# Weight splits ahead of the activation work at each feed-forward start, and two norms moved, in a two-block transformer kernel on one core

## The reference

```python
x = x + 0.5 * swiglu(rmsnorm(x, ffn1_norm[l]), w_ffn1_in[l], w_ffn1_out[l])   # hidden width 2816
x = x + mixer(rmsnorm(x, mix_norm[l]))          # block 1: MLA + HGRN2 + memory attention, gated
x = x + 0.5 * swiglu(rmsnorm(x, ffn2_norm[l]), w_ffn2_in[l], w_ffn2_out[l])   # block 2: RWKV-7 + retention
```

## Time and profile before

| | |
|---|---|
| median of 3 runs | 2368.36 us (2367.09 to 2368.44) |
| the profiled execution | 2367.09 us, of which the span of the instructions 2365.3 |
| TensorE busy | 2348.6 us |
| weight loads of TensorE (they overlap the matmuls) | 2300.9 us |
| VectorE busy | 1570.5 us |
| ScalarE busy | 1201.0 us |
| GpSimd busy | 116.5 us |
| transfers | 406.92 MB, mean 172 GB/s |

### The profile page before, as it was taken

The page is one execution under the profiler, slowest core; times in us unless marked ns, Lnnn a source line. Parts: engine busy times, 40 slices in busy tenths (PEclk is TensorE's granted clock), DMA queues, the critical chain, the costliest instruction groups (busy, mean ns, idle before and its releaser), DMA issues.

```text
span 2365.3 us, 52326 instructions
## 1 busy us (share of the span) xinstructions
PE 2348.6 (99%) x23022; PEld 2300.9 (97%) x23022; DVE 1570.5 (66%) x1416; ACT 1201.0 (51%) x1214; POOL 116.5 (5%) x74
## 2 busy tenths in 40 slices
PE   9999999999999999999999999999999999999998
PEld 8999999999999999999999999999999999999998
DVE  6766777865675568777556656866656656866655
ACT  5545655544454456565445444736445444735443
POOL 0000251000000003500000000000000000000000
PEclk9999999999999999999999999999999999999999
DMA  8656454555555554445655565513655664513653
GB/s 287 204 194 184 131 163 134 188 193 192 184 196 195 195 174 143 144 143 173 207 192 176 196 195 165 183 39 126 208 188 179 207 195 164 184 39 126 202 190 106
DMA packets 322781, 406.92 MB, mean 172 GB/s; under 512 B 6480, under 2 KB 291152, under 8 KB 322384
## 3 DMA queue, kind: packets, MB, share of 16 engines
q1 hardware_dynamic: 321488, 400.58, 52.3%
q10 hardware_dynamic: 1152, 4.22, 0.5%
HBM read 403.72 MB, written 1.05 MB: 171 GB/s over the span
## 4 chain that ended last, share of the span: by engine, by line
PE 92%; ACT 3%; DVE 3%; issue 1%; DMA 0%; SPq 0%; DVEq 0%; ACTq 0%
PE ps L339 83%; PE ps L344 8%; ACT w_hi L298 1%; DVE w_lo L303 1%; PE ps L1487 0%; DMA raw<-in_w_ffn_in 0%; DVE pad L1992 0%; DVE x_hl L392 0%; PE ps L2203 0%; ACT coef L1873 0%; ACT x_hl L366 0%; DVE x L2191 0%; DVE rms L2019 0%; ACT k_t L1132 0%; ACT kk L1842 0%
## 5 line engine op out<-in xcount | busy, mean ns | idle before, releaser
L339 PE MATMUL ps<-x_hl,w_hi 128*128 128x256 f32 x7808 | 1344.0, 277 | 2.4 <-issue 0.9
L303 DVE TENSOR_TENSOR w_lo<-raw,w_hi 128x2048 fp32r<-128x2048 f32 x383 | 881.3, 2302 | 466.5 <-ACT w_hi L298 465.8
L339 PEld LDWEIGHTS ps<-x_hl,w_hi 128*128 128x128 f32 x7808 | 1177.4, 188 | 7.0 <-issue 3.2
L339 PE MATMUL ps<-x_hl,w_lo 128*128 128x256 f32 x3904 | 1078.8, 276 | 0.0
L298 ACT CAST w_hi<-raw 128x2048 fp32r<-128x2048 f32 x383 | 731.1, 1911 | 602.6 <-PE ps L339 591.1
L339 PEld LDWEIGHTS ps<-x_hl,w_lo 128*128 128x128 f32 x3904 | 732.9, 188 | 0.0
L339 PE MATMUL ps<-h_hi,w_lo 128*128 128x256 f32 x1408 | 390.3, 277 | 0.0
L339 PE MATMUL ps<-h_hi,w_hi 128*128 128x256 f32 x1408 | 390.3, 277 | 0.0
L339 PE MATMUL ps<-h_lo,w_hi 128*128 128x256 f32 x1408 | 390.2, 277 | 0.0
L339 PEld LDWEIGHTS ps<-h_hi,w_lo 128*128 128x128 f32 x1408 | 265.2, 188 | 0.0
L339 PEld LDWEIGHTS ps<-h_hi,w_hi 128*128 128x128 f32 x1408 | 265.2, 188 | 0.0
(11 more groups left out here) (455 smaller groups left out, 2471.0 us busy)
## 6 DMA issues: line engine op xcount, KB each, us to landing
raw<-in_w_ffn_in SPq DMA_DIRECT2D x87, 1024.0 KB, 5.1
raw<-in_w_in SPq DMA_DIRECT2D x74, 1024.0 KB, 5.4
raw<-in_w_ffn_out SPq DMA_DIRECT2D x44, 1024.0 KB, 4.9
raw<-in_ffn_w_gate SPq DMA_DIRECT2D x44, 1024.0 KB, 5.3
raw<-in_ffn_w_up SPq DMA_DIRECT2D x44, 1024.0 KB, 5.3
raw<-in_ffn_w_down SPq DMA_DIRECT2D x44, 1024.0 KB, 4.9
raw<-in_w_out SPq DMA_DIRECT2D x16, 1024.0 KB, 5.2
raw<-in_w_mem_kv SPq DMA_DIRECT2D x8, 1024.0 KB, 5.0
```

What stands on the lines that cost most here:

```text
L303: nc.vector.tensor_tensor(w_lo[:, slot, :], raw[:, slot, :], w_hi[:, slot, :].bitcast(F32), ALU.subtract).then_inc(lo_ready, 1)
L339: mm = nc.tensor.matmul(out_ap, l, r, start=first and n == 0, stop=last and n == 2, skip_group_check=True)
```

## The change

Five edits of order; no arithmetic is changed.

1. ScalarE, start of each feed-forward stage: the casts of units (q+1, 0) and (q+1, 1) stand ahead of the silu and of the cast of `hid`, in place of behind them.
2. VectorE, the same place: the low split of (q+1, 0) stands ahead of `scale_silu`, that of (q+1, 1) ahead of `product`. Both stood behind `product`.
3. VectorE, end of stage 6: the low split of the next stage's second unit stands ahead of the updates of x, in place of behind them.
4. TensorE, stage 6: the norm's matmuls stand ahead of the fifth row chunk of the second projection, as in the other stages; they stood ahead of the third.
5. TensorE, mixers of block 2: the norm's matmuls stand ahead of the projection U_K, in place of in its middle.

```diff
             nc.scalar.preload_act_table_set("silu_and_others")
+            split_hi(act, q + 1, 0)
             silu(0)
-            split_hi(act, q + 1, 0)
+            split_hi(act, q + 1, 1)
             high(0, 1)
-            split_hi(act, q + 1, 1)
...
             dve.wait_ge(rms_ready, n + 1)
             take_a(0, q, 0)
+            split_lo(dve, q + 1, 0)
             scale_silu(0)
+            split_lo(dve, q + 1, 1)
             product(0, q, 1)
-            split_lo(dve, q + 1, 0)
             low(0, 1)
-            split_lo(dve, q + 1, 1)
...
-            late = (n + 1) % STAGES == 0 or n >= joint_stage
+            late = (n + 1) % STAGES == 0 or n > joint_stage
...
-                    if norm and k == (2 if n == joint_stage else DC // 2):
+                    if norm and k == DC // 2:
                         norm_pe(pe, n, 3)
...
-            project(pe, q, U_K, 256, x_hi, x_lo, DC, 256, cols2(2),
-                    first_wait=lambda i: norm_pe(pe, n) if i == DC // 2 else None)
+            norm_pe(pe, n)
+            w_in(U_K, 2)
             w_in(U_K + 1, 3)
```

## The result

The changed kernel takes 2391.09 us (median of 4 runs, 2390.07 to 2394.33) against 2368.03 for the kernel before. The ratio is 1.0100, 95% interval 1.0083 to 1.0117: **slower by 1.0%, about 23 us**. The forecast was 2385, range 2380 to 2391. Of all executions in this document one, of E8, ran at a mean granted clock of 0.948 in place of 0.99 or more; it took 2438.07 us and is left out of E8's ratio.

A forecast was written before the change was run, and what follows sets the result against it. TensorE's own stream was taken to bound the kernel, so only its waits count: 13.6 (seven starts) + 3.4 (joint stage) + 0.5 (mixers) = 17.5 us on 2367.09 gives 2384.6, forecast 2385, range 2380 to 2391.

The forecast's parts named there:

- The sum: Whole kernel: 13.6 for seven starts, 3.4 joint stage, 0.5 mixers make 17.5 us slower, bounds 15.2 and 20.8.
- The starts: Seven feed-forward starts: TensorE stalls 1.94 us each waiting for the first product, 13.6 us together.
- It holds VectorE to 1122.08: Stage 5 start: low split (q+1,1) occupies VectorE from 1119.87, so the product ends 0.69 later, at 1122.77.
- The clock: Behind TensorE's new pauses: full clock assumed; the rival had 1.2 GHz, 4.8 us lost per stage, 2423 us, chance 2%.
- The joint stage: Stage 6: stalls of about 0.9 us on `ta_done` and on the product, together 3.4 us, bounds 3.1 and 3.8.
- The mixers and the end of stage 6: Block 2 mixers and stage 6's end: new waits 0.4, 0.7, 1.4 us, bonus wait given back, net +0.5.
- The upper bound: Mixers and stage 6's end: at most +1.6 us, with nothing given back, less the chain's head start.
- the head starts of 0.5 and 0.2: Block 2's two mixers: the chain behind the earlier norm starts only 0.5 and 0.2 us earlier, not 2.7.
- The table load: Feed-forward starts: load costs 1.28 us, next activation 0.01 behind; the skill's extra 1.38 drain, 9.7 more in sum, not used.
- No stall: Feed-forward starts: product done before TensorE needs it, only the mixers' cost left, 2367 to 2369 us; chance 5%.
- the table load falls behind the cast: Feed-forward starts: chain shorter by 1.28, stalls about 0.65 us each, 7 us in sum, 2374 us; chance 5%.
- The delay reaches the chunk loop: Feed-forward chunk loops: ScalarE's casts stay late, another us lost per stage, 2393 us; chance 8%.

The follow-up runs named there:

- E8: Kernel before with only ScalarE's two casts moved ahead of the silu and the `hid` cast at feed-forward starts: 2373.54 us, ratio 1.0029.
- E3: Changed kernel plus 8 dummy matmuls of zeros ahead of TensorE's wait for the first product in each feed-forward stage: 2387.64 us, ratio 1.0084.
- E4: Kernel before with only unit (q+1,0)'s cast ahead of the silu and its low split ahead of `scale_silu`: 2369.15 us, ratio 1.0007.
- E10: Changed kernel plus 4 dummy matmuls ahead of TensorE's wait for the first product in each feed-forward stage: 2388.84 us, ratio 1.0094.
- E2: Kernel before with only the early low split ending stage 6 and the moved norms of stage 6 and the mixers: 2369.81 us, ratio 1.0010.
- E5: Kernel before with only the norm moved ahead of U_K in the two mixers of block 2: 2369.65 us, ratio 1.0011.
- E11: The changed kernel measured again, unaltered: 2394.41 us, ratio 1.0114.
- E1: Kernel before with only the casts and low splits moved ahead at feed-forward starts: 2391.75 us, ratio 1.0102.
- E9: Kernel before with feed-forward-start casts and splits moved, plus two waited-for 128x512 VectorE multiplications ahead of each stage's product: 2410.12 us, ratio 1.0176.
- E12: Kernel before with the norm ahead of U_K in block 2's mixers and 6 dummy matmuls ahead of that norm: 2369.42 us, ratio 1.0008.
- E13: Kernel before with the second pair of h tiles 320 bytes lower, at the first pair's offset: 2369.79 us, ratio 1.0008.

## Why the prediction failed

**The sum.** In the profiled execution the change costs 26.0 us where the sum had 17.5. Of the 8.5 that are missing, about 4.9 are half-clock stretches, 2.7 the mixers and the end of stage 6, 0.8 the restart behind the waits of seven starts, and 0.2 a slow spacing in stage 2. With the clock kept full (E3) the kernel takes 2387.64, which the range holds.

**The starts: the waits right, a small term missing.** The chain of cast, split, scaling, split and product was read correctly to 0.01 us, and TensorE's waits are on the product in all eight stages. E4 confirms the step of the second split, "It holds VectorE to 1122.08": with that one split behind the product no wait on it is left. Seven starts were put at 13.6 us and measured 17.8. Of the 4.2, 3.2 are two half-clock stretches, 0.8 is the restart, which the sum did not have (the second matmul behind a wait comes 0.23 later, not 0.11, so 0.12 each), and 0.2 the slow spacing in stage 2.

**The clock: this step failed.** The prediction said "The pauses in this trace reach 1.04 us, behind which the clock stayed full" and carried that over to pauses of 1.94: the sum has nothing for it, and the rival got 2%. The runs show, by length of the pause:

| pause, us | half-clock stretches | where |
|---|---|---|
| 1.1 | 0 of 7 | E10 |
| 1.47 (1.30 idle), on the squares | 0 of 7 | E2, E3, E5 twice, E10, E11, the changed kernel |
| 1.8, joint stage | 0 of 1 | E10 |
| 1.95 | 8 of 21 | E1, E11, the changed kernel |
| 2.15 to 2.66, joint stage | 2 of 3 | E1, E11, the changed kernel |
| 3.4 to 3.6 | 8 of 8 | E9 |

Filling the pause removes them all (E3). So the clock took 4.9 of the 26.0 us of the profiled execution (1.6 to 1.7 in each of three stages), and it goes with the scatter of 4 us between executions, whose mean clocks are 0.997 to 0.999; those of E3 and E10 have 0.999 to 1.000. As priced, the rival was wrong too: it had every one of the eight stages lose 4.8 us; three lost 1.6. The Trainium skill (TensorE: Matmul & The Clock Gate, Why this matters for your kernels) warns of the half clock only behind idle gaps longer than any pause of the changed kernel; the traces show the loss already behind 1.95 us, in 8 of 21 cases, and the measurement decides.

**The joint stage: right.** Forecast 3.4; measured 5.03, less a stretch of 1.6: 3.4. Both waits are there, 1.1 from start to start on `ta` and 2.59 on the product.

**The mixers and the end of stage 6: mis-sized.** Forecast +0.5, measured 3.2 in the profiled execution. The waits came much as worked out: 0.55 in front of U_LORA (0.4), 0.2 and 1.3 idle on the squares (0.7 and 1.4), and the bonus wait is gone, which gave back 2.0 (2.0). What the sum lacked is the spacing. By start of the same matmul:

| | stage 7 | stage 10 |
|---|---|---|
| up to U_K, slower spacing | +0.3 | 0 |
| the norm and its wait, up to the middle of U_K | +0.8 | +1.9 |
| from there to the bonus product, slower spacing | +1.4 | +1.0 |
| the bonus wait given back | -1.2 | -0.8 |
| behind it | -0.2 | -0.4 |

The slower spacing is 2.6 of the 3.2; the rest is 0.6, as forecast. What decides between the two spacings stays open; and E12 shows a second thing that the sum can't hold, the breaks between the short matmuls behind the bonus product, which come and go by 1 us and more from trace to trace, with the norm in its old place too (E13). The upper bound was also added up too low by its own terms: 0.4 + 0.7 + 1.4, less the head starts of 0.5 and 0.2, is 1.8 and not 1.6.

**The table load.** The trace's spacing held: the next ScalarE instruction starts 0.01 behind each of the eight loads, in all traces.

**Rivals.** "No stall" and "the table load falls behind the cast" were refuted by the waits. "The delay reaches the chunk loop" was not seen: inside the chunk loops the distance behind does not change by more than 0.15 us.

**Beating both.** Nothing did. E4, the part of the change that adds no wait on the product, is the same as the kernel before within the interval; E13 gives with one hand and takes with the other.

## What to carry to other kernels

When an engine that is 99% busy waits for a short chain, add up the chain in its written order and compare it with the work the engine has left: here, with one split moved, the product was ready 0.1 us before TensorE needed it, and the second put 2.2 us of work that TensorE did not need yet in front of it; the arithmetic gave the stall of stage 5 to 0.01 us. Prices read from short pauses don't carry over to longer ones: a stall of TensorE of 2 us can cost a stretch at half clock on top, differently in each execution, and if it can't be removed, dummy matmuls under it recover that part (3.5 of 23 us here, and half as many did nearly as well). Look for such a stretch in windows of a few us behind the longest waits; a mean over 60 us doesn't show it.

## What was not expected of the hardware

- Behind pauses of TensorE of 1.95 us the granted clock fell to its lower level in 8 of 21 cases, each for a loss of 1.6 to 1.7 us, and in other stages at each execution. In the changed kernel it fell only 0.3 to 1.4 us after TensorE had started again.
- The same 128x256 matmuls start 0.113 or 0.118 us apart, in stretches of 40 to 1590 that begin at a break of the stream. Which one follows is not set by these edits: behind the mixers' norm it was slow in the first, the second, both or none.
- The spacing of 0.120 in passes over the second h pair belongs to the tile's address (E13: 320 bytes lower it is 0.113), and in stage 6 such a pass ended a slow stretch: without it, 1596 matmuls of stage 6 took 187.97 in place of 182.12 us.
